# Stick-breaking stage: the values' differences are transposed one step later, behind the weighing

## The reference, cut to the stage in question

```python
z = jnp.einsum("bhqd,bhkd->bhqk", qb, kf[:, :, :kl]) * scale
mask = jnp.arange(kl)[None, :] < q_pos[:, None]
log_one_minus = jnp.where(mask, jax.nn.log_sigmoid(-z), 0.0)
rev = lax.cumsum(log_one_minus, axis=3, reverse=True)
weights = jnp.exp(jnp.where(mask, z + rev, -jnp.inf))
outs.append(jnp.einsum("bhqk,bhkd->bhqd", weights, vf[:, :, :kl]))
```

## Time and profile before

| | |
|---|---|
| median of 3 runs | 3250.09 us (3246.55 to 3251.26) |
| time of the profiled execution | 3245.57 us |
| its span, first to last instruction | 3242.2 us |
| the stick-breaking stage, from its first scores to its last weighing | 1195.65 to about 1641 us |
| PE busy in the whole span | 3009.9 us, 93% |
| DVE busy | 2254.7 us, 70% |
| ACT busy | 1641.8 us, 51% |
| mean granted TensorE clock | 0.974 |

### The profile page before, as it was taken

How to read it: one execution, slowest core, us unless ns; L and a number is a source line. 1 busy time by engine, 2 the same in 40 slices (tenths; PEclk the granted TensorE clock), 3 DMA queues, 4 the chain that set the end, 5 groups by cost and what they waited for, 6 DMA issues and landing times. The chain is left out here.

```text
span 3242.2 us, 48147 instructions
## 1 busy us (share of the span) xinstructions
PE 3009.9 (93%) x17460; PEld 2375.4 (73%) x17460; DVE 2254.7 (70%) x3296; ACT 1641.8 (51%) x3004; POOL 193.2 (6%) x448
## 2 busy tenths in 40 slices
PE   6999999999998989999998999999777889998799
PEld 5888788888787867777777778776655666776587
DVE  8888877754667758888877545323378889988543
ACT  5443422233545437777778232212377888888500
POOL 0000000000000000110000000000022111212100
PEclk8999999999999999999999999999889999999899
DMA  4444422245566541211155342323721111011665
GB/s 120 116 115 125 141 67 66 85 143 161 147 202 215 187 127 32 50 31 31 44 160 169 94 130 92 109 85 95 187 56 27 30 27 24 21 37 37 156 192 156
DMA packets 377859, 331.46 MB, mean 102 GB/s; under 512 B 100988, under 2 KB 331900, under 8 KB 371472
## 3 DMA queue, kind: packets, MB, share of 16 engines
q1 hardware_dynamic: 371640, 292.35, 31.8%
q0 software_dynamic: 5264, 35.72, 3.0%
q10 hardware_dynamic: 720, 0.31, 0.0%
HBM read 211.26 MB, written 107.10 MB: 98 GB/s over the span
## 5 line engine op out<-in xcount | busy, mean ns | idle before, releaser
L629 PE MATMUL p_oa_acc<-s_h_a_hi,s_mx_w_hi 128*128 128x512 f32 x768 | 301.8, 393 | 13.4 <-DVE s_h_a_lo L418 9.4
L323 ACT ACTIVATE s_mx_w_hi<-s_mx_raw 128x512 fp32r<-128x512 f32 x224 | 139.0, 629 | 319.4 <-PE p_oa_acc L629 255.6
L629 PE MATMUL p_oa_acc<-s_h_a_hi,s_mx_w_lo 128*128 128x512 f32 x768 | 300.7, 392 | 0.0
L629 PE MATMUL p_oa_acc<-s_h_a_lo,s_mx_w_hi 128*128 128x512 f32 x768 | 300.6, 391 | 0.0
L1598 DVE TENSOR_TENSOR_SCAN s_st_prod<-s_st_soft,s_st_prod 128x512 f32<-128x512 f32 x192 | 234.3, 1266 | 17.6 <-ACT s_st_soft L1525 17.6
L3125 PE MATMUL p_sa_turn<-s_ident,s_sa_arg 128*128 128x128 f32 x1088 | 168.5, 292 | 47.2 <-ACT s_sa_prob L2752 35.1
L1525 ACT ACTIVATE s_st_soft<-p_st_z 128x512 f32<-128x512 f32 (+3 forms) x320 | 153.7, 534 | 113.1 <-PE p_st_z L1650 113.1
L2340 PE MATMUL p_pr_ps<-s_h_hi,s_pr_w_hi 128*128 128x512 f32 (+1 forms) x712 | 195.6, 395 | 11.0 <-ACT s_pr_stage L2187 8.8
L2340 PE MATMUL p_pr_ps<-s_h_lo,s_pr_w_hi 128*128 128x512 f32 (+1 forms) x712 | 193.0, 392 | 0.0
L460 DVE TENSOR_TENSOR s_mx_w_lo<-s_mx_raw,s_mx_w_hi 128x512 fp32r<-128x512 f32 x224 | 153.2, 684 | 56.1 <-ACT s_mx_w_hi L323 54.6
L2340 PE MATMUL p_pr_ps<-s_h_hi,s_pr_w_lo 128*128 128x512 f32 (+1 forms) x712 | 191.6, 389 | 0.0
(11 more groups left out here) (376 smaller groups left out, 7407.1 us busy)
## 6 DMA issues: line engine op xcount, KB each, us to landing
s_mx_raw<-in_w_in_a SPq DMA_DIRECT2D x128, 256.0 KB, 3.7
s_pb_ada<-in_w_ada SPq DMA_DIRECT2D x16, 768.0 KB, 4.3
s_pr_raw<-in_w_in SPq DMA_DIRECT2D x21, 512.0 KB, 3.8
s_pr_work<-s_pr_stage SPq DMA_DIRECT2D x38, 256.0 KB, 4.8
d_rot_hi<-s_pr_rot POOLq DMA_DIRECT2D x9, 1024.0 KB, 4.3
d_rot_lo<-s_pr_stage POOLq DMA_DIRECT2D x9, 1024.0 KB, 6.2
d_p_t<-s_pr_stage POOLq DMA_DIRECT2D x9, 1024.0 KB, 8.2
d_y_t<-s_mx_y SPq DMA_DIRECT2D x16, 512.0 KB, 5.4
```

Of the source, the lines that this page charges most:

```text
L323: nc.scalar.activation(w_hi[:, m], raw[g % 2][:, m], ACT.Copy).then_inc(hi_done, 1)
L629: ins = nc.tensor.matmul(bank, w[:, m, k, :], a[:, m, k, :], start=(k == 0 and n == 0), stop=(k == KH - 1 and n == 2))
```

## The change

In all three places that order the chores' transposes, `chores_at(t - 1)` becomes `chores_at(t - 2)`: in the list `turns`, in ACT's loop and in PE's. On PE `transpose_v` also moves behind `weigh`. Nothing is added or removed; the 64 transposes and the 16 copies stay.

```diff
-        for n, _, _ in chores_at(t - 1):
+        for n, _, _ in chores_at(t - 2):
             turn_of["v", n] = len(turns)
             turns.append(("v", n))
...
-                for c in chores_at(t - 1):
+                for c in chores_at(t - 2):
                     leave_v(*c)
...
-                for c in chores_at(t - 1):
-                    transpose_v(*c)
                 if 0 <= t - 1 < U:
                     weigh(t - 1)
+                for c in chores_at(t - 2):
+                    transpose_v(*c)
```

## The result

The changed kernel takes 3254.96 us (median of 11 runs, 3250.93 to 3259.03) beside 3249.16 of the kernel before (11 runs, 3246.24 to 3251.84): a ratio of 1.0019, 95% interval 1.0010 to 1.0027. It is **slower by 5.8 us**, a little under the 0.2% that the prediction set as its bound; but the sum had said -0.2, and the interval of 3.2 to 8.8 us excludes that. A second set of 11 runs on another occasion gave 3254.30 and 1.0018 (1.0009 to 1.0027). The profiled execution took 3253.18 us with a span of 3250.9.

The account below looks back on a forecast made before the run. PE, busy 93% of the span, was taken to bound the kernel. Terms of +2.1 (fourth chores), -2.3 (third), +0.5 (first), -0.1 (second) and -0.4 (opening) summed to -0.2 us: 3249.9 us from 3250.09, range 3243 to 3256.

Parts of the forecast that it names:

- the 0.2% that the prediction set as its bound: Whole kernel: a measurement can tell about 0.2%, 6.5 us, from no change.
- the sum: Whole change: +2.1 - 2.3 + 0.5 - 0.1 - 0.4 = -0.2 us, giving 3249.9 us.
- What bounds, and where the waits go: PE, 93% busy, sets the pace; moved transposes' 13.8 us of waits go, units' transposes wait 12 to 15 for scans.
- The rival in which they simply vanish: Stage's PE waits: all go and none comes back, -13.8 us to 3236.3; chance 0.03.
- that of DVE setting the pace at all 16 chores: Every chore, as at the fourth: each costs 0.52 us, +8.3, 3258.4, slower; chance 0.03.
- The terms of first, second and third chore: Next scores' start: first +0.18 us each (pairs 1 to 3), second -0.04 (pairs 1 to 3), third -0.57 (4 times).
- The fourth chores, +0.52 each: Fourth chore of each pair: scans hold head 1, values' transposes now lie behind; next scores +0.52 us each, +2.1 in all.
- The opening, -0.4: Two chores of pair 0: DVE's chain comes about 0.9 us earlier, half of it given back; -0.4 us taken.
- The bounds, -1.7 to +1.0: Opening: from -1.68 us, the whole PE wait, to +1.0, four more transposes at the low clock and nothing won.
- The 0.9 that DVE's chain was to come earlier: Opening: the first copy leaves ACT's queue ahead of the second chore's `k_hi`; DVE's chain comes about 0.9 us earlier.
- The rival of the other clock: Opening, 6 us at clock 0.50: denser work gives 3246.9 us (chance 0.12), or new gaps 3253 (chance 0.07).
- The forecast of no change: Whole kernel: same within about 0.2%, chance 0.92; faster 0.04, slower 0.04.

Follow-up runs that it names:

- The filled waits: The changed kernel with 48 dead identity transposes on PE ahead of the waits for the scans behind each fourth chore; 3250.18 us, ratio 1.0005.

## Why the prediction was right or wrong

**What bounds, and where the waits go: right.** PE's waits left the moved transposes and came back at the next unit's, 12.2 us against 12 to 15 forecast. The rival in which they simply vanish is out; so is that of DVE setting the pace at all 16 chores, since the third chores gained.

**The terms of first, second and third chore: right** to 0.06 us each, against the table. The rule behind them is that head 1 starts 0.15 us after its scans end. In the rows of pair 2's fourth chore the scans end at 1463.40 + 2.45 = 1465.85, and head 1 starts at 1466.00; at the first chore of pair 1 they end at 1295.78 + 2.45 = 1298.23, and it starts at 1298.38.

**The fourth chores, +0.52 each: the step that failed.** The sum took it that a wait costs its own length and nothing else, so that a wait moved from ahead of the values' transposes to behind the scores cost only the 0.52 of work that it no longer covered. It costs more, since it does not come alone: of one wait of 1.31 with work behind it, the change makes two, 1.24 and 0.55, with four transposes between, and behind that the clock fell to 0.50 in three of four cases. The term measured 2.19, 2.14, 0.52 and 2.13, together 7.0 for 2.1. The filled waits show that it is the idleness and not the lateness. Why one pair of waits brings a fall and a like or longer one doesn't stays open, beyond that it depends on when they come; no run set out to fill only one of the two waits. In one case, pair 1 with the waits filled, a single wait of 1.26 us was left and the clock stayed; so it isn't shown whether their closeness or their sum counts. The prediction named the clock, but gave it a place (the opening) and a direction (denser work, 3 us less, or more gaps) without asking where the change itself makes PE idle in a new pattern. The rule of the Trainium skill that it quoted there (Perfetto Trace Analysis, section Matmul Optimizations: back to back, since power follows utilization) would have been a rival for the fourth chores; there the runs agree with it, by the 1.6 to 1.7 us that dead work gave back at each of three fourth chores.

**The opening, -0.4: the direction right, the size uncertain.** It is -1.75 between the first two profiles, and some -1.5 in the mean of all, with a scatter larger than that. The bounds, -1.7 to +1.0, just hold the mean. The 0.9 that DVE's chain was to come earlier is there in every profile, as 1.0. The rival of the other clock made the low stretch a matter of the change; the runs show it ending at different times in one and the same kernel.

**The sum.** -0.2 was forecast; the fourth chores add 4.9 and the opening takes 1.35, which gives the stage's +3.9 (the small differences of the other terms make up the rest). The measured 5.8 is 1.9 more, within its interval of 3.2 to 8.8; the time without the opening, +5.9, is closer. Whether the timed runs show less of the opening's gain than the profiles is open: they have no trace each.

**The numbers.** 3254.96 lies in the range of 3243 to 3256, and the move is within 0.2%. The forecast of no change was still wrong: the interval of the ratio lies wholly above 1.

## What to carry to other kernels

When an edit on PE only moves a wait, look for the chain that ends the wait; here it was DVE's share of a chore, which itself idled for ACT, and moving that share behind the urgent scans won 15 us where moving the transposes lost 5.8. Of any new wait on PE ask not only how long it is but what stands directly before and after it: behind two short waits close together the clock fell here in three of four places, and the work behind them took up to 1.7 times as long. A dead filler in the wait is a cheap test of that.

## What the runs showed of the hardware

That 1.8 us of idleness on PE, in two pieces with 0.5 us of transposes between, brought the granted clock from 1.00 to 0.50 was not expected. A single wait of 1.31 never did, in 15 cases in the five profiles with the fourth chores in their old place, nor did the 1.31, 0.43 and 0.55 us of pair 1's fourth chore in the same five; nor, once, 1.76 and 0.55 with the same transposes between. Each fall cost 1.6 to 1.7 us beyond the 0.52 of work. Whether it comes depends on when the waits lie: dead work that shifted pair 2 by 1.1 us moved the spared fall from pair 2 to pair 3. And at the opening of the stage, behind 7.3 us of idleness, the clock returned to 1.00 for good at anything from 1207 to 1214 us in the profiles of one and the same kernel, which makes the stage 444.8 to 447.4 us long.
